# Modulation products of a two-layer model on TensorE, with the conditions as stationary operand, and a first norm that takes its scales chunk by chunk

## The reference, cut to what matters

```
silu_c = jax.nn.silu(c)
silu_cc = jax.nn.silu(c_ctx)
for l in range(DEPTH):
    ctx_out = l < DEPTH - 1
    mod = silu_c @ w_ada[l] + b_ada[l]
    sh_a, sc_a, g_a, sh_f, sc_f, g_f = jnp.split(mod[:, None, :], 6, axis=-1)
    n_c = 6 * d if ctx_out else 2 * d
    mc = jnp.split(silu_cc @ w_ada[l][:, :n_c] + b_ada[l][:n_c], n_c // d)
    hx = rmsnorm(x) * (1 + sc_a) + sh_a
    hc = rmsnorm(ctx) * (1 + mc[1]) + mc[0]
    ux = hx @ w_in[l]
    ...
```

## Time and profile before

| | us |
|---|---|
| median of 3 runs (lowest, highest) | 4628.94 (4620.43, 4631.04) |
| profiled execution | 4612.46 |
| its span | 4611.2 |
| PE busy in it | 4006.7 (87%) |
| DVE busy | 2124.5 (46%) |
| ACT busy | 1339.6 (29%) |
| mean granted PE clock | 0.924 of full speed |

### The profile page before, as it was taken

The page is one execution under the profiler, slowest core; times in us unless marked ns, Lnnn a source line. Parts: engine busy times, 40 slices in busy tenths (PEclk is TensorE's granted clock), DMA queues, the critical chain, the costliest instruction groups (busy, mean ns, idle before and its releaser), DMA issues.

```text
span 4611.2 us, 45961 instructions
## 1 busy us (share of the span) xinstructions
PE 4006.7 (87%) x18748; PEld 3232.0 (70%) x18748; DVE 2124.5 (46%) x3323; ACT 1339.6 (29%) x1796; POOL 211.2 (5%) x324
## 2 busy tenths in 40 slices
PE   7987655899998967469998999967999899898998
PEld 6855444788887845357886886735888688676886
DVE  6536666564624246654334334265333433444334
ACT  2114433311112225333223223344222322323222
POOL 0000132000000000210000000000000000000000
PEclk8889877999998989679999999978999999999999
DMA  4310000132411210002222222201222222221222
GB/s 190 137 69 1 9 0 1 73 119 105 152 64 55 73 41 9 0 28 83 100 93 82 95 97 83 98 4 37 92 100 101 73 101 92 82 92 64 101 94 80
DMA packets 47743, 342.31 MB, mean 74 GB/s; under 512 B 5376, under 2 KB 5376, under 8 KB 7728
## 3 DMA queue, kind: packets, MB, share of 16 engines
q1 hardware_dynamic: 37728, 275.80, 16.6%
q0 software_dynamic: 8768, 61.49, 3.6%
q10 hardware_dynamic: 1040, 2.10, 0.1%
HBM read 337.26 MB, written 2.10 MB: 74 GB/s over the span
## 4 chain that ended last, share of the span: by engine, by line
PE 79%; DVE 11%; ACT 5%; POOL 3%; issue 2%; DMA 0%; ACTq 0%; DVEq 0%; POOLq 0%
PE PS L333 59%; PE PS L335 6%; PE PS L1166 3%; PE PS L862 2%; PE PS L834 2%; DVE SQ L425 2%; POOL E L1142 1%; DVE RS L773 1%; PE PS L374 1%; PE PS L783 1%; PE PS L848 1%; ACT WZ L1263 1%; POOL E L1143 1%; PE PS L721 1%; PE PS L393 1%
## 5 line engine op out<-in xcount | busy, mean ns | idle before, releaser
L310 DVE TENSOR_TENSOR WL<-raw,WH 128x2048 fp32r<-128x2048 f32 x260 | 595.9, 2292 | 434.6 <-ACT WH L305 434.6
L305 ACT ACTIVATE WH<-raw 128x2048 fp32r<-128x2048 f32 x260 | 495.4, 1906 | 462.7 <-PE PS L333 346.6
L1166 PE MATMUL PS<-WZ,E 128*128 128x256 f32 x560 | 165.9, 459 | 183.2 <-ACT WZ L1263 169.1
L333 PE MATMUL PS<-XH_ff,WH 128*128 128x512 f32 x704 | 280.7, 399 | 12.3 <-DVE XL_ff L436 12.3
L333 PE MATMUL PS<-XH_b,WH 128*128 128x512 f32 x704 | 277.0, 394 | 11.7 <-DVE XL_b L436 10.3
L333 PE MATMUL PS<-XH_a,WH 128*128 128x512 f32 x704 | 277.0, 393 | 11.6 <-DVE XL_a L436 10.2
L1166 PEld LDWEIGHTS PS<-WZ,E 128*128 128x128 f32 x560 | 125.7, 232 | 221.6 <-ACT WZ L1263 186.1
L333 PE MATMUL PS<-XH_ff,WL 128*128 128x512 f32 x704 | 277.2, 394 | 0.0
L333 PE MATMUL PS<-XL_ff,WH 128*128 128x512 f32 x704 | 277.1, 394 | 0.0
L333 PE MATMUL PS<-XH_a,WL 128*128 128x512 f32 x704 | 275.4, 391 | 0.0
L333 PE MATMUL PS<-XL_a,WH 128*128 128x512 f32 x704 | 275.3, 391 | 0.0
(11 more groups left out here) (345 smaller groups left out, 8757.6 us busy)
## 6 DMA issues: line engine op xcount, KB each, us to landing
raw<-in_panels SPq DMA_DIRECT2D x260, 1024.0 KB, 4.7
ada_ff<-in_ada_panels POOLq DMA_DIRECT2D x24, 1024.0 KB, 5.0
ada_win<-in_ada_panels POOLq DMA_DIRECT2D x16, 1024.0 KB, 5.0
ada_start<-in_ada_panels POOLq DMA_DIRECT2D x8, 1024.0 KB, 24.4
FX<-in_dft_x POOLq DMA_DIRECT2D x2, 2048.0 KB, 8.1
X<-in_xT SPq DMA_DIRECT2D x1, 3072.0 KB, 10.9
out<-X ACTq DMA_DIRECT2D x1, 2048.0 KB, 7.0
WZ<-in_masks POOLq DMA_DIRECT2D x2, 896.0 KB, 5.0
```

Source lines behind the costliest of these rows:

```text
L305: H.up(ac.activation(WH[s].rearrange("p k n -> p (k n)"), raw[:, s, :], ACT.Copy), n)
L310: L.up(ve.tensor_tensor(WL[s].rearrange("p k n -> p (k n)"), raw[:, s, :], WH[s].bitcast(F32).rearrange("p k n -> p (k n)"), ALU.subtract), n)
L333: t = te.matmul(PS[:, j, :], lhsT, x[:, k, 0:SEQ], start=st, stop=end)
L1166: t = te.matmul(PS[:, k, fc * 2 * P:(fc + 1) * 2 * P], b["E"][d][:, lv, fc, :], b["WZ"][d][:, lv - g0, fc].rearrange("p h n -> p (h n)"), ...
```

## The change

Every panel of `w_ada` now takes one way, in two steps on PE. In `te_ada_parts` the two conditions are the stationary operand, padded with zeros to 32 columns (`cv` is 128 x 8 x 32), and the panel's chunk is the moving one, 256 columns. Chunk k goes to the group of 32 columns, and so to the 32 PSUM partitions, number k mod 4. Four partial sums lie on the partitions 0, 32, 64, 96 (and 1, 33, 65, 97 for the context). They are copied to SBUF (`ve_ada_parts` at the start, `ac_ada_parts` on ACT elsewhere), and `te_ada_sum` adds the four with a product of two columns for each 128 features, a 0/1 matrix in `HM[:, 2:4]` as the moving operand. The bias instruction adds the scales' 1 too. DVE's terms, the direct way and `ve_one_plus` are gone.

At the start the panels are read as 0, 4, 1, 5, ..., so that shift and scale of two chunks come together, and the norm begins with the first pair; `ve_start_chunks` runs ahead of the norm's even chunks. The panels 6 and 7 of that order lie in the two slots of `wi0`'s ring, and POOL issues the later ones as PE's reads free these, without the fence behind the start.

```diff
-    cv = keep.take("cv", [P, NC, 2])
-    HM = keep.take("HM", [P, 2])
+    cv = keep.take("cv", [P, NC, 32])
+    HM = keep.take("HM", [P, 4])
...
-        def ve_normed(name, XH, XL, ctx, gain, shift):
+        def ve_normed(name, XH, XL, ctx, gain, shift, ahead=None):
             ve.wait_ge(*A[(name, "RS")])
 
             def scale(c):
+                if ahead:
+                    ahead(c)
...
+        def te_ada_parts(name, panel, ring, landed, m):
+            te.wait_ge(*landed[(name, panel)])
+            wait_bank(4 + m % 2)
             for k in range(NC):
...
+                g = slice(k % 4 * 32, k % 4 * 32 + 32)
+                t = te.matmul(PS[g, 4 + m % 2, 0:2 * P], cv[:, k, :], ring[:, k, :], start=k < 4, stop=k >= 4,
+                              skip_group_check=True)
+            T.up(t, (name, "parts", panel))
+
+        def te_ada_sum(name, panel, AD, m, by):
+            te.wait_ge(*by[(name, "parts", panel)])
+            wait_bank(6 + m % 2)
             for j in range(2):
...
+                t = te.matmul(PS[:, 6 + m % 2, 2 * j:2 * j + 2], AD[m % 2][:, j * P:(j + 1) * P], HM[:, 2:4],
+                              start=True, stop=True)
             T.up(t, (name, "ada", panel))
...
+        def ac_ada_parts(name, panel, AD, m):
+            ac.wait_ge(*T[(name, "parts", panel)])
...
+            A.up(ac.activation(AD[m % 2][:], PS[:, 4 + m % 2, 0:2 * P], ACT.Copy), (name, "parts", panel))
...
+            V.up(ve.scalar_tensor_tensor(mod[:, l, p * 2:p * 2 + 2, 0:n],
+                                         PS[:, 6 + m % 2, 0:4].rearrange("p (a b) -> p a b", a=2)[:, :, 0:n],
+                                         1.0 if scales else 0.0, bias, ALU.add, ALU.add),
+                 (name, "mod", panel), (name, "mods"))
...
-        plans = {(1, True): ("F0 F1", "V0", "V1 S0", "", "S1"),
-                 (2, True): ("F0 F1", "V0 F2", "V1 S0 F3", "S1 V2", "S2 T3"),
-                 (2, False): ("F0 F1", "V0 F2", "V1 S0 F3", "S1 V2 V3", "S2 S3")}
+        plans = {1: ("P0", "S0", "P1", "S1", ""), 2: ("P0", "S0 P1", "S1 P2", "S2 P3", "S3")}
...
+        def gp_ada_all(name, b, start, n, slots_used):
+            for m in range(n):
+                back = T[(name, "parts", start + m - 2)] if m >= 2 else slots_used[m] if slots_used else None
+                gp_ada(name, b["ada"][m % 2], ada_landed[m % 2], start + m, back)
...
+        START = [0, 4, 1, 5, 2, 6, 3, 7]
...
-            for s in range(0, 8, 2):
-                if s == 2:
-                    ve_stats("wi0", True)
-                ve_ada_terms("st", ring_start, AD_start, s, s)
-                ve_ada_bias("st", s + 1, 3)
-                ve_ada_bias("st", s, 4)
-            ve_one_plus("st.sc", 0, SC_A)
+            for s in range(2):
+                ve_ada_parts("st", START[s], mix1[0]["AD"], s)
+            ve_stats("wi0", True)
+
+        def ve_start_chunks(c):
+
+            if c % 2 == 0:
+                for s in (c, c + 1):
+                    ve_ada_bias("st", START[s], s)
+                for s in (c + 2, c + 3):
+                    if s < NC:
+                        ve_ada_parts("st", START[s], mix1[0]["AD"], s)
+                ve.wait_ge(*V.now())
...
-            for s in range(0, 8, 2):
-                if s == 2:
-                    te_stats("wi0", True, True)
-                te_ada_direct("st", ring_start, s + 1, s + 1, 3)
-                te_ada_sum("st", AD_start, s, s)
...
+            parts(0)
+            parts(1)
+            te_stats("wi0", True, True)
+            for s in range(NC):
+                te_ada_sum("st", START[s], mix1[0]["AD"], s, V)
+                if s % 2:
+                    for x in (s + 1, s + 2):
+                        if x < NC:
+                            parts(x)
```

More of the change, by code:

```diff
@@ L170, in program @@
     shelf = Shelf(first)
-    ring_start = shelf.take("ada_start", [P, 8, NC, 2 * P])
-    AD_start = [shelf.take(f"AD{s}_start", [P, 2, 2 * P]) for s in range(2)]
+    ring_start = [shelf.take(f"ada_start{s}", [P, NC, 2 * P]) for s in range(6)]
     mix1 = []
@@ L470, in te_halves, with gp_ada @@
             return lambda k: te.wait_ge(*V[(name, "XL", k)])
-        def gp_ada(name, ring, slot, panel, back=None):
+        def gp_ada(name, into, signal, panel, back=None):
             if back:
                 gp.wait_ge(*back)
[L477 to L484, removed]
-            for k in range(NC):
[L486 to L495, removed]
@@ L504, in te_ada_direct @@
             T.up(t, (name, "ada", panel))
[L505 to L516, removed]
@@ L543, in ada_steps, with te_ada @@
                 return []
             return [(what[0], int(what[1]), start + (p // 2) * 2 * rounds + int(what[1]))
-                    for what in plans[rounds, both][x].split()]
-        def te_ada(name, b, start, rounds, both=True):
+                    for what in plans[rounds][x].split()]
+        def te_ada(name, b, start, rounds):
             def beside(p, j):
-                for what, m, panel in ada_steps(start, rounds, both, p, j):
+                for what, m, panel in ada_steps(start, rounds, p, j):
+                    if what == "P":
+                        te_ada_parts(name, panel, b["ada"][m % 2], ada_landed[m % 2], m)
+                        bank(4 + m % 2, A, name, "parts", panel)
+                    else:
+                        te_ada_sum(name, panel, b["AD"], m, A)
+            return beside
@@ L550, in beside, with ac_ada, ve_ada @@
+        def ac_ada(name, b, start, rounds):
+            def beside(p, j):
+                for what, m, panel in ada_steps(start, rounds, p, j):
+                    if what == "P":
+                        ac_ada_parts(name, panel, b["AD"], m)
+            return beside
+        def ve_ada(name, start, rounds, n=2):
+            def beside(p, j):
+                for what, m, panel in ada_steps(start, rounds, p, j):
                     if what == "S":
-                        te_ada_sum(name, b["AD"], m % 2, panel, both)
@@ L565, in gp_ada_all @@
[L565 to L571, removed]
-                                direct = rounds == 2 and both and (before - start) % 4 == 3
-                                back = T[(name, "ada", before)] if direct else V[(name, "terms", before)]
-                            gp_ada(name, b["ring"], m % 2, panel, back)
+                        ve_ada_bias(name, panel, m, n)
@@ L585, in gp_start @@
             const_landed.up(gp.dma_start(HM[:], head_mask), "all")
-            for s in range(8):
-                gp_ada("st", ring_start, s, s)
+            for s, panel in enumerate(START):
+                gp_ada("st", ring_start[s], start_landed[s], panel)
         def ac_start():
```

115 lines of the change are left out of this document (54 added, 61 removed).

## The result

| | before | after |
|---|---|---|
| median of four runs (lowest, highest) | 4627.49 (4620.43, 4631.04) | 4663.6 (4658.68, 4668.24) |
| span of the profiled execution | 4611.2 | 4659.8 |
| mean granted PE clock | 0.924 | 0.928 |

A forecast was written before the change was run, and what follows sets the result against it. PE was taken as the bound (79% of the chain, DVE 11%). Start 12, projection 12.3, ff0 -39.0 and one-plus 0.5 sum to 14.2 us slower: 4627 profiled, 4643 as median, range 4585 to 4712.

The forecast's parts named there:

- The wider cv and head mask: Transfers at the start: 128 KB and 2 KB, ahead of X, PE waiting for the head mask as now; cost nothing.
- P: On PE, each panel's partial sums, eight 256-column products on four column groups: 2.13 us, bounded by 0.9 and 3.6.
- Rival B: At each P, column groups run fully side by side, P 0.9 to 1.1: 42 us faster, 4587; chance 0.27.
- lower bound of 0.9: P if all four column groups run side by side: 4 x 0.225 us.
- S: On PE, each panel's sum, two products of two columns (4 records): 0.36 us.
- First projection: Accumulators m = 1 to 17: 150.1 + 15 P against 194.4 us, 12.3 gained at P 2.13.
- Start: Up to the copy of m = 0: norm starts at 45.9, m = 0 ends near 73.4 against 87.9; 12 gained.
- The clock that I priced at 2.3: At the start, matmuls run partly at the lower clock, as they do now; 2.3 us taken off the gain.
- ff0: First feed-forward stage: 24 x 0.36 + 23 P against 18.6 us, 39.0 lost at P 2.13.
- C: Rival: column groups do not overlap, P = 3.6; 77 us slower, 4706; chance 0.24.
- D: Rival: as C, and the clock falls, each accumulator behind P losing about 1.5 us, 60 more; 4766; chance 0.05.
- E: Rival: the start does not get shorter, PE's rounds replacing DVE's, so the 12 are missing; 4655; chance 0.02.

The follow-up runs named there:

- e2: The changed kernel with 64 unused bytes per partition behind the head mask, so later tiles lie 1024 bytes further than before: 4594.6 us, ratio 0.9935.
- e1: The kernel before with only 960 unused bytes per partition behind the head mask, placing later tiles as in the changed kernel: 4701.42 us, ratio 1.0171.
- e6: e2 with the products in the order 0, 4, 1, 5, 2, 6, 3, 7, two in a row on one column group: 4586.81 us, ratio 0.9918.
- e5: e2 with all eight products of a panel on one group of 32 columns, copies and sum on 32 partitions: 4714.15 us, ratio 1.0193.
- e3: The kernel before with four added products of 32 stationary and 256 moving columns at its start, one per column group: 4627.57 us, ratio 1.0.
- e11: The kernel before with 256 unused bytes per partition behind the head mask, shifting the moving tiles: 4617.21 us, ratio 0.9987.
- e12: The kernel before with 128 unused bytes ahead of the weight tiles, so weight and moving tiles both lie 128 bytes further: 4619.0 us, ratio 1.0.
- e4: The changed kernel with the 64 bytes of e2, and ff0 the old way (terms on DVE, one-column sums on PE): 4580.86 us, ratio 0.9908.
- e7: The kernel before with 64 unused bytes ahead of WH and 64 behind the head mask; weights 64, moving tiles 128 bytes further: 4651.27 us, ratio 1.0063.
- e8: The kernel before with 64 unused bytes behind the head mask, so the moving tiles lie 64 bytes further: 4650.04 us, ratio 1.0052.

## Why the prediction was right in sign and wrong in reason

**The failed step** is the last part of the sum: "The wider cv and head mask are 128 KB and 2 KB [...] and PE waits for the head mask at 15.88 as now: nothing", and with it "All else the same to a few us". I priced the wider tile as a transfer and not as a layout. What it moved costs 69 us (after against e2; e1 has 78 for the same shift on the kernel before). No rival had it either. Without it the sign would have been wrong: 29 us faster, where I gave 0.33 to faster. That the 36 us measured and the 14 forecast have the same sign is an accident.

**P.** The term was mis-sized: 1.00 measured, 2.13 forecast. Rival B's mechanism is the true one. My lower bound of 0.9, four steps of 0.225 from the earlier trace rows, missed by 0.1, the share that I had put on getting into and out of the shape. I chose the middle of the bounds by the argument that records start in program order, and e6 shows that it does not carry to column groups. The Trainium skill ("TensorE: Matmul & The Clock Gate", Part 3, Measured speedup vs the span model) has 2.38x for three column tiles, which is 0.79 of the number of tiles. No run here has three; four give 3.57x (P of e5 against that of e2), 0.89 of the number. By the page's figure the prediction had an estimated 13 us faster, the right sign for the bare change. Entering the shape has a price outside of P, too: S takes 0.07 more where a P follows (0.43 or 0.44 against 0.36), so that entering and leaving cost at most some 0.17 together, where the sum had 0.1. The Trainium skill ("TensorEngine Tiling (Array Packing)", Key Properties) states that changing the tiling mode drains TensorE; the trace here agrees in so far as it has room for a drain of that length and none longer.

**First projection.** From the copy of m = 0 to the last copy before took 194.4 and takes 167.5: 26.9 gained, forecast 12.3. The formula 150.1 + 15 P gives 165.1 with the measured P, 2.4 under the measured time. It was right but for P; of the 2.4, S is about 1 (15 of 16 stand ahead of a P, at 0.43 and not 0.36).

**Start.** m = 0 is copied out 21.0 earlier; forecast 12, and 21 in rival B. The norm starts at 42.37, not 45.9: 2.3 of the difference is P (0.97 each for 2.13), 1.2 that the products on SS take 1.47 and not 2.70. DVE waits 1.02 for P in the first round, at 41.91, and 0.61 in the second, at 47.07, so the rounds in which PE holds up DVE are there, and short. (87.9 less 73.4 is 14.5 and not the 14.3 of the prediction; nothing hangs on it.) The clock that I priced at 2.3 does fall (0.57 from 38.2 to 48) and doubles two pairs of P.

**ff0.** It took 594.8 and takes 619.0: 24.2 lost, forecast 39.0. By P and S alone it is 24 x 0.44 + 23 x 1.00 = 33.6 against 18.6, 15 lost. The pace makes the rest: e1, the kernel before on the shifted layout, takes 602.9 there (908.38 to 1511.28). So at the layout of after the change costs 16.1. The layout costs 8.1 by before against e1, and less by the other kernels that have the code of before and distance 0 (597.3 in e3, 598.9 in e11, 599.2 in e12).

**The sum of the bare change.** With P = 1.00 and the measured start, my sum is 21 + 29.3 - 13.0 + 0.5 = 38 faster. Two pairs of kernels measure it: e2 against before, 29 faster (22 to 38), and after against e1, both at distance 192, 4701.42 - 4663.6 = 38 faster (42 by the two ratios). So with P put right the sum holds as well as these runs can tell.

What blurs them is the stretch between the last copy of the first projection and the first product of `wo0`. It takes 526.5 us in before and 537.8 in after (234.50 to 772.26), the 11.3 that the lead shrinks there. That is neither the change nor the layout: e11 and e12 run the code of before at distance 0 and have one length each. The view by stretches of before, after, e11 and e12:
```profile
282.36:808.86 526.50, 326.80 (x1606) 241.14 (x1607) 316.59 (x729) 196.77 (x370) 82.53 (x135) 0.82 0.03 9
```
```profile
234.50:772.26 537.76, 337.96 (x1606) 247.68 (x1607) 316.20 (x728) 196.84 (x370) 82.55 (x135) 0.79 0.03 9
```
```profile
283.08:820.19 537.11, 337.60 (x1606) 247.28 (x1607) 316.46 (x729) 196.74 (x370) 82.56 (x135) 0.79 0.03 9
```
```profile
285.16:812.20 527.04, 327.56 (x1607) 241.71 (x1607) 316.40 (x729) 196.67 (x370) 82.45 (x135) 0.82 0.03 9
```
PE with its weight loads is busy longer, for the same instructions, and no other engine is, while the granted clock is 0.79 instead of 0.82. Why it is granted less in some executions is open. The waits for DVE are gone, as forecast, and ACT's copies cost PE nothing that shows.

**C, D and E** fell: groups run side by side, the record behind P is at 0.50, the start is shorter. C's slope was nearly right for a kernel without groups, and its price low: e5, with a P of 3.57 and the layout of e2, is 91 us slower than before, where C had 77.

## What to carry to other kernels

When a tile grows in a memory laid out in sequence, look at what it moves: compare the step between matmuls of an untouched stage before and after, and if it differs, pad until the weight and moving tiles stand at the old distance modulo 256 bytes. Small products with 32 stationary columns are worth spreading over the four column groups; the two orders tried were equally good. Work that hides on a waiting engine beside dense matmuls should not go onto the engine that sets the time, even where it is cheap there (e4), while the same work at a start where PE itself waits is worth moving.

## What the runs showed of the hardware that I had not expected

- The step between consecutive 512-column float32r products depends on the distance in SBUF of stationary and moving tile, with a period of 256 bytes: 0.2267, 0.2289, 0.2324 to 0.2333 and 0.2333 us for 0, 64, 128 and 192 bytes, and up to 78 us of 4624 with it. Only multiples of 64 were tried, and only float32r. Tiles between the two moved too in e7 and e12.
- At distance 64 the records differ in length, and not by kind of product: in e8 the stages on XH_a have 398 ns with WH and 392 with WL, as shown above, and those on XH_b the other way round. What decides which product is the long one is open.
```profile
L334 PE MATMUL PS<-XH_b,WL 128*128 128x512 f32 x704 | 278.3, 395 | 0.0
...
L334 PE MATMUL PS<-XH_b,WH 128*128 128x512 f32 x704 | 275.8, 392 | 12.4 <-DVE XL_b L437 10.4 <-POOL XL_b L454 2.0
```
- Up to some 1550 us the products come as a pair of 512 and 256 columns, and there distance 0 is not a guarantee. On the mean the pair takes 0.347 us at the fast pace and 0.353 at the slow one. The kernel before is mostly slow up to 900 us and again from 1500, e2 is in part of ff0, and e4 in nearly all of it; after and e1, at distance 192, are slow throughout. Why is not known.
- Four column groups turn eight fp32 products of 256 columns from 3.57 into 1.00 us; two or four records of a group in a row make next to no difference (1.00 and 1.02).
- The same code, with the same layout modulo 256 bytes, takes 527 or 537 us between the first projection and `wo0`, at a granted clock of 0.82 or 0.79 (e12 and e11). A difference of 10 us between two traces of this kernel can be that alone.
